# A fused diffusion step on one core: rearranged passages between its three stages, and short runs of products of ones in three places of each

## The reference

```
h = adaln_in(x, g[0], sh(0), sh(1))
x = x + 0.5 * sh(2) * rmsnorm(swiglu(h, p['w_gate'][0], p['w_up'][0], p['w_down'][0]), g[1])
h = adaln_in(x, g[2], sh(3), sh(4))
mix, new_ml, new_ssm = hybrid_mixer(h, p, ml_state, ssm_state, n_seg)
x = x + sh(5) * rmsnorm(mix, g[3])
h = adaln_in(x, g[4], sh(6), sh(7))
x = x + 0.5 * sh(8) * rmsnorm(swiglu(h, p['w_gate'][1], p['w_up'][1], p['w_down'][1]), g[5])
```

## Time and profile before

| | us |
|---|---|
| median of three runs | 3108.17 (3106.86 to 3108.97) |
| profiled execution | 3105.14 |
| its span, first to last instruction | 3103.3 |
| PE busy | 3001.2 (97%) |
| POOL, VectorE, ACT busy | 1830.1, 1328.4, 971.1 |

### The profile page before, as it was taken

One profiled execution on the slowest core, in us unless ns is written; L12 is line 12 of the kernel. 1 busy time (PEld: TensorE's weight loads), 2 busy tenths in 40 slices (PEclk: granted clock), 3 DMA queues, 4 the chain that ended last, 5 costly groups with the idle time before them and its releaser, 6 DMA issues.

```text
span 3103.3 us, 46282 instructions
## 1 busy us (share of the span) xinstructions
PE 3001.2 (97%) x16569; PEld 2760.5 (89%) x16569; DVE 1328.4 (43%) x2849; ACT 971.1 (31%) x1259; POOL 1830.1 (59%) x908
## 2 busy tenths in 40 slices
PE   6999999999999996899999999799999999999998
PEld 2799999999999995799999988699999999999997
DVE  3365566555755663486753353513342111100113
ACT  2322322222223223433432233532222322232223
POOL 2565655666656654456865446566555666666666
PEclk8999999999999998899999999899999999999999
DMA  9866765666656673865544445245554554444443
GB/s 363 279 214 208 226 211 189 203 210 217 211 188 211 211 234 111 216 189 149 148 134 115 127 114 190 68 128 187 173 166 142 154 147 127 129 127 123 128 128 109
DMA packets 472269, 535.73 MB, mean 173 GB/s; under 512 B 37595, under 2 KB 401603, under 8 KB 470723
## 3 DMA queue, kind: packets, MB, share of 16 engines
q1 hardware_dynamic: 427904, 512.82, 52.7%
q10 hardware_dynamic: 44227, 21.30, 2.9%
HBM read 523.31 MB, written 9.69 MB: 172 GB/s over the span
## 4 chain that ended last, share of the span: by engine, by line
PE 89%; DVE 3%; DMA 2%; issue 2%; POOL 2%; ACT 1%; ACTq 1%; DVEq 0%; SPq 0%; POOLq 0%
PE banks L802 19%; PE banks L804 19%; PE banks L803 19%; PE banks L919 9%; PE banks L921 9%; PE banks L920 9%; DVE HB L2264 1%; POOL w_lo L2541 1%; PE banks L833 1%; DMA w_raw<-in_w_ada_dram 1%; DMA g_wait<-coefG 1%; PE banks L1277 0%; PE banks L1297 0%; ACTq L1501 0%; DMA w_raw<-in_ffn_w_gate_dram 0%
## 5 line engine op out<-in xcount | busy, mean ns | idle before, releaser
L2541 POOL TENSOR_TENSOR w_lo<-w_raw,w_hi 128x1024 fp32r<-128x1024 f32 (+1 forms) x668 | 1596.9, 2396 | 1032.2 <-ACT w_hi L1370 1032.1
L802 PE MATMUL banks<-xn_hi,w_hi 128*128 128x384 f32 x3664 | 1248.3, 341 | 13.4 <-POOL w_lo L2541 12.0
L803 PE MATMUL banks<-xn_lo,w_hi 128*128 128x384 f32 x3664 | 1229.7, 336 | 0.0
L804 PE MATMUL banks<-xn_hi,w_lo 128*128 128x384 f32 x3664 | 1229.6, 336 | 0.0
L1370 ACT ACTIVATE w_hi<-w_raw 128x1024 fp32r<-128x1024 f32 (+1 forms) x668 | 703.9, 1056 | 1493.1 <-PE banks L804 646.3
L802 PEld LDWEIGHTS banks<-xn_hi,w_hi 128*128 128x128 f32 x3664 | 691.7, 189 | 37.6 <-issue 20.3
L803 PEld LDWEIGHTS banks<-xn_lo,w_hi 128*128 128x128 f32 x3664 | 691.9, 189 | 4.2 <-issue 2.9
L804 PEld LDWEIGHTS banks<-xn_hi,w_lo 128*128 128x128 f32 x3664 | 691.5, 189 | 0.0
L1835 DVE SCALAR_TENSOR_TENSOR banks<-w_raw,cT,banks 128x256 f32<-128x256 f32 x1372 | 546.0, 482 | 0.0
L919 PE MATMUL banks<-w_hi,hid_hi 128*128 128x512 f32 x1056 | 412.9, 391 | 11.2 <-DVE y L1989 11.2
L921 PE MATMUL banks<-w_lo,hid_hi 128*128 128x512 f32 x1056 | 412.2, 390 | 0.0
(11 more groups left out here) (276 smaller groups left out, 1556.3 us busy)
## 6 DMA issues: line engine op xcount, KB each, us to landing
w_raw<-in_w_ada_dram SPq DMA_DIRECT2D x288, 512.0 KB, 5.8
w_raw<-in_ffn_w_gate_dram SPq DMA_DIRECT2D x176, 512.0 KB, 4.1
w_raw<-in_ffn_w_up_dram SPq DMA_DIRECT2D x176, 512.0 KB, 4.1
w_raw<-in_ffn_w_down_dram SPq DMA_DIRECT2D x176, 512.0 KB, 4.0
w_raw<-in_w_in_dram SPq DMA_DIRECT2D x104, 512.0 KB, 3.7
w_raw<-in_w_out_dram SPq DMA_DIRECT2D x32, 512.0 KB, 3.7
HB<-row_wait ACTq DMA_DIRECT2D x12, 512.0 KB, 4.5
AM<-g_wait SPq DMA_DIRECT2D x4, 1024.0 KB, 9.5
```

Source lines behind the costliest of these rows:

```text
L802: pe.matmul(out, wh, hi, start=start, stop=False)
L803: pe.matmul(out, wh, lo, start=False, stop=False)
L804: return pe.matmul(out, w_lo[:, w, off:off + P], hi, start=False, stop=stop)
L2541: pool.tensor_tensor(used(w_lo[:, slot(p), :], p), used(w_raw[:, p % NR, :], p), used(w_hi[:, slot(p), :], p).bitcast(F32), ALU.subtract). ...
```

## The change

- **Gains of FFN 1.** The loop of ten is written as a loop of three and one of seven with the same body (part "more"); `gate_coefs(0)` on VectorE and `store_gains(0)` on ACT stand between them. `load_gains` stays where it was.
- **`w_ada` in passage 0.** Four of the sixteen pieces (PASS_PIECES) are multiplied right after the last products. The other twelve, with the twelve that stood among the gate pieces anyway, now follow one behind each main piece from M2 on. In the list of loads they stand in this order too; before, it was three main pieces, the sixteen, and the rest.
- **Products of ones.** `stay_awake(n)` makes n products of ones by ones, 128 columns each, now into bank 7: 4, 8 and 8 in passage 0, and 24, 8 and 8 in passage 1 (WAKE): before the turns, before the last spread, and before the first main piece. Before, all counts were zero.
- **Order in the passages.** In `end_of`, `finish` of block (1, 2) moves behind `add_last` and `root_bias` of (2, 3), in all three stages. ACT squares (y, 2, 3) before (x, 1, 2). Of the three `make_hi` and `make_lo` among the squares and gains one is left on POOL and ACT, M1's `make_hi` comes behind the squares, and the others stand between the tiles (HI_ORDER, LO_ORDER).
- **Gains of passage 1.** `store_gains(1)` moves from behind the last tile of passage 0 to main piece M17.

```diff
-FFN_PARTS = [[("first", 0, 1), ("loop", 1, FFN_IT - 1)], ...
+PASS_PIECES = 4
+FFN_PARTS = [[("first", 0, 1), ("loop", 1, 3), ("more", 4, FFN_IT - 4)], ...
-GATE_PIECES = spread([...], MIX_ADA, 2 * U * "m" + ADA_MIX * U * "am" + (XBC_T // 2 - ADA_MIX - 1) * U * "m")
+MIX_ADA = [("a", 0, q) for q in range(PASS_PIECES, 4 * ADA_PASS)] + [("a", ADA_PASS + k, q) for k in range(ADA_MIX) for q in range(U)]
+GATE_PIECES = spread([...], MIX_ADA, "mm" + len(MIX_ADA) * "ma" + (U * (XBC_T // 2 + 1) - 2 - len(MIX_ADA)) * "m")
+GATE_PIECES = [("a", 0, q) for q in range(PASS_PIECES)] + GATE_PIECES
-WAKE = ((0, 0), (0, 0))
+WAKE = ((4, 8, 8), (24, 8, 8))
+HI_ORDER = (((2, range(5)), (3, range(5, 8)), (4, range(8, 11)), (5, range(11, 14)), (None, range(14, KT))),
+            ((2, range(5)), (3, range(5, 8)), (4, range(8, 11)), (None, range(11, KT))))
-                        pe.matmul(psum[0][:, 0:P], ones[:, :], ones[:, :], start=True, stop=True)
+                        pe.matmul(psum[7][:, 0:P], ones[:, :], ones[:, :], start=True, stop=True)
+                def passage(stage):
+                    stay_awake(WAKE[stage][0])
+                    for k in range(2):
+                        turn(stage, k)
+                    for c in range(2):
+                        spread_root(stage, c)
+                    stay_awake(WAKE[stage][1])
+                    spread_root(stage, 2)
+                    for k in range(2, TURN_AHEAD):
+                        turn(stage, k)
+                    stay_awake(WAKE[stage][2])
-                    if n == 0:
-                        store_gains(0)
+                        if n == 0 and part == "loop":
+                            store_gains(0)
-                store_gains(1)
+                    if (n, q) == (3, 1):
+                        store_gains(1)
-                    finish(stage, 1, 2)
                     add_last(stage, 2, 3)
                     root_bias(stage, "y", 2)
+                    finish(stage, 1, 2)
                     finish(stage, 1, 3)
```

More of the change, by code:

```diff
@@ L108, in sum_events @@
     for kind, s, q in ffn_pieces(n, part):
[L109 removed]
+        together = n == 0 and part in TOGETHER
         if kind == "b" and q == U - 1 and (not together or s == ADA_STEPS[part] - 1):
@@ L574, in ada_unit @@
         def ada_unit(n, part, k):
-            return {"first": ADA_FIRST, "loop": UNIT_LOOP, "early": UNIT_LATE}[part] + k
+            return {"first": ADA_FIRST, "loop": UNIT_LOOP, "more": UNIT_LOOP + 3 * ADA_STEPS["loop"], "early": UNIT_LATE}[part] + k
         def summed(unit):
@@ L1343, in _ @@
                             head_out(*of)
[L1344 to L1352, removed]
+                passage(1)
                 ffn(1)
@@ L1516, in _ @@
                 ffn(0)
-                for p, tiles in zip(GATE_FIRST, (range(8), range(8, 12), range(12, 14))):
+                for m, tiles in HI_ORDER[0]:
                     hi_of(1, tiles)
-                    make_hi(ahead(p))
-                hi_of(1, range(14, KT))
+                    if m is not None:
+                        make_hi(MAIN[M_OF[GATE_FIRST[0]] + m])
                 act.dma_start(x_wait, AX).then_inc(x_spilled, 16)
-                store_gains(1)
                 def gate_part(m):
@@ L1736, in _ @@
                 for name, c, cc in SQUARES[1][9:]:
[L1737 to L1739 removed]
                     square_block(1, name, c, cc)
[L1741 to L1747 removed]
+                    if (name, c, cc) == ("y", 1, 3):
+                        make_hi(FFN2)
+                make_hi(FFN2 + 1)
+                for m, tiles in HI_ORDER[1]:
+                    hi_of(2, tiles)
+                    if m is not None:
+                        make_hi(FFN2 + m)
                 ffn(1)
@@ L1803, in pre_norm @@
                     for k in range(KT + 2):
-                        if stage == 1 and k == 10:
-                            ada_rows_out(next(p for p, *piece in GATE_STEPS if piece == ["a", 0, 4 * ADA_PASS - 1]), UNIT_MIX)
                         if k < KT:
@@ L2639, in _ @@
                 ffn(0)
-                for p, tiles in zip(GATE_FIRST, ((0, 2, 4, 6), (8, 10), (12,))):
+                for m, tiles in LO_ORDER[0]:
                     even_low(1, tiles)
-                    make_lo(ahead(p))
-                even_low(1, (14,))
+                    if m is not None:
+                        make_lo(MAIN[M_OF[GATE_FIRST[0]] + m])
                 for p, kind, n, q in GATE_STEPS:
@@ L2727, in _ @@
                     if (c, cc) == (2, 3):
-                        make_lo(ahead(P_MIX + S_LAST + 1))
-                        make_lo(ahead(P_MIX + S_LAST + 2))
+                        make_lo(FFN2)
                     gain(1, c, cc)
-                make_lo(ahead(P_MIX + S_LAST + 3))
-                even_low(2, range(0, 8, 2))
-                make_lo(ahead(FFN2))
-                even_low(2, range(8, 12, 2))
-                make_lo(ahead(FFN2 + 1))
-                even_low(2, range(12, KT, 2))
+                for m, tiles in LO_ORDER[1]:
+                    even_low(2, tiles)
+                    if m is not None:
+                        make_lo(FFN2 + m)
                 ffn(1)
```

82 lines of the change are left out of this document (27 added, 55 removed).

## The result

| | us |
|---|---|
| before, median of 5 runs beside it | 3106.86 (3105.75 to 3108.97) |
| changed, median of 5 runs | 3091.48 (3089.89 to 3093.47) |
| ratio, 95% interval | 0.995 (0.9936 to 0.9964) |
| span of the profiled execution | 3089.7, before 3103.3 |
| forecast | 3079.3 (3073 to 3089) |

What follows compares the result with a forecast made beforehand. PE was taken to be busy 97% of the span, leaving only idle time and half clock in the passages to win. Terms 14.2 + 13.0 - 1.7 + 5.1 - 4.3 + 4.0 + 0.4 - 1.8 = 28.9 us gave 3079.3 us (3073 to 3089).

Steps and rivals of the forecast that it cites:

- What bounded the kernel: Whole kernel: PE busy 97% of the span; only its idle time in the passages and half clock behind it can be won.
- the end of FFN 1: FFN 1's last blocks: early-stored gains end PE's wait for adds; products end at 1208.7 instead of 1222.8, 14.2 us won.
- a sign of being wrong: End of FFN 1: gains taking over 3 us would show the forecast wrong; it had three of them at 1.9 us.
- To the spread of chunk 2: Passage 0, from FFN 1's last product: w_ada waits and two of three make_lo leave; 13.0 us won (11 to 14.5).
- To the first product: Passage 0, from the spread: eight more products of ones between turns 3 and 4; 1.7 us lost (1.0 to 3.2).
- First product to M7: From M0's first product to M7's end: M6's stall goes, M5's stays, five w_ada pieces are added; 5.1 us won.
- up to 1 us: At M1 in passage 0: loss allowed because its w_lo now comes after tiles 0 and 2.
- The other pieces of w_ada: After M7: seven more pieces at 0.55 and one set of columns at 0.43, unhidden; 4.3 us lost.
- The moved stores: Stores 0 and 1 of gains slow loads beside them: 0.3 and 1.5 us, together 1.8 us lost (0 to 6).
- Passage 1 and the end: Mixer to FFN 2: 4.0 us won (2 to 5), stall at FFN 2's fifth piece stays; kernel's end: 0.4 us (0 to 1).
- POOL in the way of the gains: Rival, end of FFN 1: POOL's w_lo slows the three gains, 4.4 us lost, 3084 us; chance 0.14.
- Ones that don't pay: Rival, both passages: ones don't raise the clock, each set of eight costs 3.6 us, 3085 us; chance 0.10.

Runs made afterwards that it cites:

- the last experiment: Changed kernel with the old order of squares, finishes, w_hi and w_lo, middle store of gains behind the last tile, no products of ones: 3107.06 us.
- the kernel with the gate rows later: Changed kernel with two of VectorE's parts of the gate rows moved behind the copies of w_ada's sums: 3082.55 us, ratio 0.9931.
- With the sixth pieces too: Changed kernel with two gate-row parts behind the copies and each passage's sixth piece split ahead of the last tiles: 3074.79 us, ratio 0.9898.

## Why the prediction was wrong, point by point

**What bounded the kernel, and the end of FFN 1: right.** The gains, their loads and the adds fell as forecast: gains_first ran from 1191.04 to 1194.5, beside POOL (3.50 us for three, 1.90 alone in the earlier trace rows). That is over the 3 us which the prediction had named as a sign of being wrong, and still the add of (0, 1) was in time. Alone the term gave 13 us. Of 14.2 us 13.3 are there; a wait of 0.9 us for w_lo in FFN 1's loop, between 400 and 500 us, is the store's price, for which I had taken 0.3.

**To the spread of chunk 2: right,** 13.1 for 13.0. Its cause was put right too: two of three make_lo gone and no loads in the way, and the last experiment gives 12 to the loads. The ones did hold the spread at half clock to +15.9, as said; in another execution, with the first eight nearly at full clock, it came at +14.5.

**To the first product: 0.9 us too cautious.** The last eight ran at full clock, 1.95 us.

**First product to M7: 2.9 for 5.1.** M6's stall went, M5's stayed at 2.77, both as forecast, and no half clock stood behind it. The failed part is M1: "up to 1 us" was 2.20 us of wait and, in this execution, about 1.5 of half clock. VectorE's remainder of tile 3 (L1778, two operations with two inputs in SBUF each) took 3.06 us beside POOL's new make_lo; that of tile 5, with no POOL operation beside it, took 0.73 at 1236.42:

```profile
1231.53 2.38 POOL L2528 TENSOR_TENSOR w_lo<-w_raw,w_hi 128x1024 fp32r<-128x1024 f32 x1
1232.13 3.06 DVE L1778 SCALAR_TENSOR_TENSOR xn_lo<-AM,modT,xn_hi 128x128 fp32r<-128x128 f32 x2
```

I had priced the new piece as a delay of POOL alone. The Trainium skill (SBUF — State Buffer, "Who interferes with whom") has a VectorE instruction with two SBUF inputs contend with a GpSimd one that reads SBUF; by that rule the new make_lo had VectorE in its price, and this trace agrees with it: the first of the two operations took 1.93 us and ended 0.15 us behind the make_lo.

**The other pieces of w_ada: the step that failed.** Forecast -4.3, and -1.5 for the store; measured -20.5. Its working was "seven more at 0.55 and one set of columns at 0.43 follow in the stream, and nothing hides them, since PE is full there". It counted what PE issues and what the loads need, and took VectorE's copy ahead of each set of columns as free. The measured parts:
- idle: 6.69 and 2.43 us at the two copies (the gaps from one start to the next, less the normal spacing), 1.44 us at the store: 10.6 us;
- half clock behind the copies: from the first columns to the end of the main piece behind them 8.1 us instead of the 5.35 of the kernel with the gate rows later, from the second 6.9 instead of 5.25: 4.4 us;
- seven pieces of w_ada: the cycle of a main piece is 4.91 us with one and 4.20 without, so 0.71 each, not 0.55, since the products at its edges start later too: 5.0 us, and 0.4 for the columns.

That is 20.4 of the 20.5. Of it 13.5 us stand at the copies, and for these the prediction had no term at all. Moving two parts of VectorE's row work, with nothing else changed, gave back 8.9 us in the medians and 8.0 in this stretch of the trace, after the longer wait at the store was paid. So the cause is shown, not inferred.

**The moved stores: right in size by luck.** Store 1 cost 1.4 us, as taken, but only because the copies had delayed PE by 13 us on its way there. The load behind it took 22.0 us, not the 15 or 18 of the prediction; rounding and make_lo add 3.5, and PE came to the piece 24.3 us after the issue, which leaves the 1.3 us of wait. With the copies in order PE came after 20.2 us and the load took 20.7: 4.11 us. With the sixth pieces too it was 20.2 and 23.2: 6.57 us. Where a state's load stands behind the store, it was 14.3.

**Passage 1 and the end: right,** 4.4 us for 4.1 at the spread, 5.2 for the 4.0 of the whole term, and 0.6 for 0.4. The stall at FFN 2's sixth piece stayed, as forecast; that it is avoidable was not asked.

**The rivals.** POOL in the way of the gains: blocked, but without harm, since they started early. Ones that don't pay: none of the runs shows a gain from them in passage 0, though not for the reason named; the last eight do run at full clock. The case that happened, another engine's older work ahead of a small copy that PE needs, had no rival and no chance. Everything above 3089 us had 0.06.

## What to carry to other kernels

Before pieces of work are moved, list for each what every engine does for it, the smallest copy too, and look on that engine's timeline for what will stand ahead of it at the new place: two copies of 0.42 us, behind 13 and 9 us of unrelated work, cost as much as the early store had won. A gain ahead of a fixed transfer is kept only as far as the loads there allow; look at the next store or load that PE will meet sooner. And one profiled execution against another does not settle a few us of clock: the same instructions in passage 0 took 45.1 us in one and 48.2 in another.

## What the runs showed of the hardware

- A store of 4096 four-byte packets takes 18 us with little beside it. Loads issued up to 10 us behind such a store landed after 19.4 to 23.4 us in six traces; the median of a piece of w_in in the changed kernel is 3.8. With the store cut into two halves 29 us apart, PE waits for no piece there.
- Half clock doesn't follow from the length of a wait alone: behind the same wait of 2.2 us at tile 3 of passage 0, in the same code, five executions have it (in the changed kernel nine starts 0.32 us apart instead of 0.17) and two have not. Behind 2.26 us at 1337.3 the next 24 products took 6.01 us instead of 4.44, behind 2.77 us at 1257.8 they took 4.46. The runs don't settle the rule.
- Eight products of ones took 3.62 us in one execution and 2.25 in another at the same place; the next eight took 1.95 in both.
